# Dilated attention on one Trainium2 core: queries and keys split once for each head pair and sequence, with strided queries and keys laid by token mod 16

## What is computed

```python
DILATED_PATTERNS = ((128, 1), (512, 4), (2048, 16))

def dilated_window_attention(q, k, v, window, dilation):
    r = window // (2 * dilation)          # 64 for each of the three
    ...                                   # every dilation-th token forms a subsequence
    scores = jnp.einsum('nbqhd,nbkhd->nbhqk', qb, kw) * (HEAD_DIM ** -0.5)
    valid = (|qi - ki| <= r) & (ki >= 0) & (ki < l_sub)
    lse = jax.nn.logsumexp(scores, axis=-1)
    p = jnp.exp(scores - lse[..., None])
    o = jnp.einsum('nbhqk,nbkhd->nbqhd', p, vw)
    ...

def dilated_mixture(q, k, v):
    ...
    w = jax.nn.softmax(jnp.stack(lses, axis=0), axis=0)
    return jnp.sum(w[..., None] * jnp.stack(outs, axis=0), axis=0)
```

## Time and profile before

| | |
|---|---|
| median of 3 runs | 4136.37 us |
| lowest, highest | 4117.97, 4144.95 us |
| the profiled execution | 4143.03 us |
| its span, mean granted TensorE clock | 4141.0 us, 0.933 |
| TensorE busy over the span (products) | 3880.3 us, 94% |
| VectorE, ScalarE, GpSimd busy | 2095.0, 1547.7, 1498.9 us |
| attention, first score product to last output product | 2364.2 to 3490.6 us |

### The profile page before, as it was taken

The page is one execution under the profiler, slowest core; times in us unless marked ns, Lnnn a source line. Parts: engine busy times, 40 slices in busy tenths (PEclk is TensorE's granted clock), DMA queues, the critical chain, the costliest instruction groups (busy, mean ns, idle before and its releaser), DMA issues. The chain is left out here.

```text
span 4141.0 us, 62154 instructions
## 1 busy us (share of the span) xinstructions
PE 3880.3 (94%) x24989; PEld 3348.6 (81%) x24989; DVE 2095.0 (51%) x3847; ACT 1547.7 (37%) x2855; POOL 1498.9 (36%) x796
## 2 busy tenths in 40 slices
PE   6999999899889999999999799999999997799998
PEld 5877777677668998998988688888888886588887
DVE  2101278887324443444444355666656553467775
ACT  3323222121103222222222355777767664233322
POOL 1211155776553443343433433444433332211110
PEclk9999999999999999999999877999979885899999
DMA  6444245767533335334443223443334333454442
GB/s 233 134 158 174 83 150 189 277 219 269 171 120 112 117 105 194 110 117 146 149 122 110 88 64 101 120 122 106 94 102 122 91 83 105 151 185 172 178 181 107
DMA packets 431313, 582.99 MB, mean 141 GB/s; under 512 B 26155, under 2 KB 346739, under 8 KB 425395
## 3 DMA queue, kind: packets, MB, share of 16 engines
q1 hardware_dynamic: 425267, 562.23, 42.4%
q0 software_dynamic: 3456, 12.58, 0.7%
q10 hardware_dynamic: 2304, 4.20, 0.3%
HBM read 369.09 MB, written 209.83 MB: 140 GB/s over the span
## 5 line engine op out<-in xcount | busy, mean ns | idle before, releaser
L225 POOL TENSOR_TENSOR project_w_lo<-project_raw,project_w_hi 128x1024 fp32r<-128x1024 f32 (+1 forms) x204 | 434.8, 2141 | 1083.5 <-ACT project_w_hi L216 1083.5
L1668 ACT ACTIVATE attn_p_sb<-attn_p_sb,attn_o_sb 128x256 f32<-128x256 f32 (+1 forms) x1152 | 450.9, 464 | 335.7 <-DVE attn_o_sb L1703 335.6
L1634 PE MATMUL attn_o_ps<-attn_v,attn_pt_sb 128*128 128x65 f32 x3840 | 565.3, 305 | 0.0
L1634 PEld LDWEIGHTS attn_o_ps<-attn_v,attn_pt_sb 128*128 128x128 f32 x3840 | 522.4, 217 | 36.2 <-DVE attn_pt_sb L1713 2.7
L1713 DVE COPY attn_pt_sb<-attn_pt_ps 128x1024 f32<-128x1024 f32 (+1 forms) x288 | 301.5, 1047 | 376.8 <-PE attn_pt_ps L1618 376.7
L1703 DVE CUSTOM_DVE_ANT_0 attn_p_sb<-attn_mask,attn_s_ps 128x256 f32<-128x256 bf16 (+1 forms) x1152 | 363.9, 372 | 118.3 <-PE attn_s_ps L1606 117.2
L285 PE MATMUL third_out<-project_w_hi,project_h_hi 128*128 128x256 f32 x2304 | 373.9, 305 | 24.2 <-PEq L687 14.4
L285 PEld LDWEIGHTS third_out<-project_w_hi,project_h_hi 128*128 128x128 f32 x2304 | 301.6, 191 | 93.0 <-issue 84.9
L285 PE MATMUL third_out<-project_w_lo,project_h_hi 128*128 128x256 f32 x2304 | 326.6, 285 | 0.0
L285 PE MATMUL third_out<-project_w_hi,project_h_lo 128*128 128x256 f32 x2304 | 324.6, 284 | 0.0
L1510 POOL TENSOR_TENSOR attn_k_lo<-attn_nat,attn_k_hi 128x1024 fp32r<-128x1024 f32 (+1 forms) x96 | 199.5, 2078 | 338.0 <-ACT attn_k_hi L1658 337.9
(11 more groups left out here) (189 smaller groups left out, 6926.5 us busy)
## 6 DMA issues: line engine op xcount, KB each, us to landing
project_raw<-w_in SPq DMA_DIRECT2D x156, 512.0 KB, 5.9
output_parts<-s_o SPq DMA_DIRECT2D x24, 1584.0 KB, 6.5
s_o<-attn_o_sb SPq DMA_DIRECT2D x256, 132.0 KB, 2.0
s_xbcT<-first_stage SPq DMA_DIRECT2D x72, 256.0 KB, 2.1
project_h_hi<-s_h SPq DMA_DIRECT2D x8, 2048.0 KB, 8.9
project_h_lo<-s_h SPq DMA_DIRECT2D x8, 2048.0 KB, 13.7
s_xb<-second_toks SPq DMA_DIRECT2D x30, 512.0 KB, 6.7
second_xb<-s_xb SPq DMA_DIRECT2D x24, 640.0 KB, 9.9
```

Of the source, the lines that this page charges most:

```text
L225: last = nc.gpsimd.tensor_tensor(low, src, high.bitcast(F32), ALU.subtract)
L1634: last = nc.tensor.matmul(o_ps[n % 2][:, x, :], pt_sb[n % 2][:, x, b * P:(b + 1) * P], v[st.buf][:, st.chunk(r, t, b), half * VW:(half + 1 ...
L1668: last = nc.scalar.activation(cut, cut, ACT.Exp, scale=-1.0, bias=o_sb[n % ring][:, x % 2, x // 2, VW:OW])
```

## The change

Queries and keys are split once for each pair and sequence, 6 parts of 1024 tokens a pair, and all three dilations read the same split. For that the order becomes pair, sequence, dilation. The split queries lie in the order of the tokens, and a product takes them as its stationary operand with a stride of 1, 4, 16 or (short sequence, dilation 16) 8 elements. The split keys lie by token modulo 16 (`RHO`), 16 rows of 64 or 128 tokens with 16 of padding at either side; a product reads them as its moving operand in runs of 8 (dilation 1), 32 (dilation 4), 64 or 128 elements (dilation 16). So the keys of a block come in another order than before, and the masks (8 strips instead of 5) and the rows of the values follow it: the values of a banded stretch are loaded in 16 transfers, of 8 partitions each for dilation 1 and of 32 for dilation 4. The store of the short sequence at dilation 16 is one transfer. The splits of a sequence of the next pair are placed in the steps 1, 3, 5, 7 of the 12 steps of the short sequence, those of the pair's own short sequence at steps 4 and 8 of the long sequence. `load_nat` moves to the step i = 3 of dilation 16, behind the `load_v` of i = 2. TensorE waits for `a_low` only at the first step of a pair and sequence. The diff, cut to its core:

```diff
     def strip(self, t):
         if not self.banded:
-            return 3 + self.halves - 1
-        return 0 if t == 0 else 2 if t == self.tiles - 1 else 1
-
-    def query_at(self, r, t):
-        return (r * self.tiles + t) * P
-
-    def key_at(self, r, t):
-        return r * (self.tiles * P + 2 * self.pad) + t * P
+            return 6 + self.halves - 1
+        return 3 * self.pattern + (0 if t == 0 else 2 if t == self.tiles - 1 else 1)
+
+    def queries(self, q, rows, r, t):
+
+        step = self.dil // self.halves
+        by_sub = q[rows, :].rearrange("p (m r) -> p r m", r=step)
+        return by_sub[:, r, t * P:(t + 1) * P] if self.banded else by_sub[:, t, :]
+
+    def keys(self, k, rows, r, t):
+
+        if not self.banded:
+            own = k[rows, :, KPAD:KPAD + self.length // RHO].rearrange("p (h r) n -> p r h n", h=self.halves)
+            return own[:, t, :, :]
+        n = P * self.dil // RHO
+        first = KPAD + t * n - n // 2
+        own = k[rows, :, first:first + 2 * n].rearrange("p (q r) (b n) -> p r b q n", r=self.dil, b=2)
+        return own[:, r, :, :, :]
 
...
 def attention_stretches():
     stretches, first = [], 0
     for pair in range(PAIRS):
-        for pattern in range(len(DILATIONS)):
-            for s in (1, 0):
+        for s in (1, 0):
+            for pattern in range(len(DILATIONS)):
                 stretches.append(Stretch(len(stretches), pair, s, pattern, first))
...
+class Part:
+
+
+    def __init__(self, number, pair, s, which, half):
+        self.number, self.pair, self.s, self.which, self.half = number, pair, s, which, half
+        self.first = which == 0 and half == 0
+
+    def cut(self, t):
+
+        size = SEQS[0]
+        if self.which == 0:
+            return t[:, self.half * size:(self.half + 1) * size].rearrange("p (n r) -> p r n", r=1)
+        n = size // RHO
+        return t[:, :, KPAD + self.half * n:KPAD + (self.half + 1) * n]
+
+    def source(self, nat):
+        size = SEQS[0]
+        return nat[:, self.which, self.half * size:(self.half + 1) * size].rearrange(
+            "p (n r) -> p r n", r=RHO if self.which else 1)
+
+
+def attention_parts():
+    parts = []
+    for pair in range(PAIRS):
+        for s in (1, 0):
+            for which in range(2):
+                for half in range(SEQS[s] // SEQS[0]):
+                    parts.append(Part(len(parts), pair, s, which, half))
+    return parts
...
+        firsts = {(st.pair, st.s): st for st in stretches if st.pattern == 0}
+        ready = {}
         splits_at = [[] for _ in steps]
-        for st, following in zip(stretches, stretches[1:]):
-            for piece in range(pieces):
-                splits_at[max(0, st.first - 2 + piece * (2 if st.steps > pieces else 1))].append((following, piece))
+        for part in parts:
+            ready[(part.pair, part.s)] = part.number + 1
+            at = part.half + part.which * SEQS[part.s] // SEQS[0]
+            if part.s == 0:
+                splits_at[firsts[(part.pair, 1)].first + 4 + 4 * at].append(part)
+            elif part.pair:
+                splits_at[firsts[(part.pair - 1, 0)].first + 1 + 2 * at].append(part)
...
+            def narrow(strip, base, by_query, by_key):
+                pool.wait_ge(sem["a_mask_steps"], len(done) + 1)
+                dims = by_key + [[0, 1]] * (3 - len(by_key))
+                width = dims[0][1] * dims[1][1] * dims[2][1]
+                cut = mask[:, strip, 0:width].rearrange("p (b q n) -> p b q n", b=dims[0][1], q=dims[1][1])
+                nc.gpsimd.affine_select(out=cut, in_=cut, compare_op=ALU.is_ge, fill=BIG, base=base, pattern=dims,
                                         channel_multiplier=by_query).then_inc(sem["a_mask_steps"], 1)
-            cuts = (mask[:, 0, 0:BAND], mask[:, 2, 2 * P - BAND:2 * P], mask[0:BAND, 4, BAND:P], mask[BAND:P, 4, 0:BAND])
-            for n, cut in enumerate(cuts):
-                pool.wait_ge(sem["a_mask_steps"], len(rules) + 1 + n)
-                nc.gpsimd.memset(cut, BIG).then_inc(sem["a_mask_steps"], 1)
-            c["a_mask_total"] = len(rules) + 1 + len(cuts)
+                done.append(strip)
+
+            done = []
+            for pattern in range(2):
+                q, n = RHO // DILATIONS[pattern], P * DILATIONS[pattern] // RHO
+                after_key = [[P, 2], [1, q], [q, n]]
+                before_key = [[-P, 2], [-1, q], [-q, n]]
+                for strip in range(3 * pattern, 3 * pattern + 3):
+                    narrow(strip, 0, -1, after_key)
+                    narrow(strip, P, 1, before_key)
+                narrow(3 * pattern, -BAND, 0, after_key)
+                narrow(3 * pattern + 2, P + BAND - 1, 0, before_key)
+            narrow(6, BAND, -1, [[1, P]])
+            narrow(6, BAND, 1, [[-1, P]])
+            c["a_mask_total"] = len(done) + 1
...
                     reach = BAND * st.dil
-                    rows = cut[base - reach:base + st.length + reach, :].rearrange("(t p r) n -> r p t n", p=P, r=st.dil)
+                    m = P * st.dil // RHO
+                    rows = cut[base - reach:base + st.length + reach, :].rearrange(
+                        "(t m q r) n -> r q m t n", q=RHO // st.dil, m=m, r=st.dil)
                     for r in range(st.dil):
                         at = r * (st.tiles + 1)
-                        sp.dma_start(v[st.buf][:, at:at + st.tiles + 1, :], rows[r]).then_inc(sem["a_v_in"][st.buf], 16)
+                        for q in range(RHO // st.dil):
+                            sp.dma_start(v[st.buf][q * m:(q + 1) * m, at:at + st.tiles + 1, :], rows[r, q]
+                                         ).then_inc(sem["a_v_in"][st.buf], 16)
                 else:
-                    rows = cut[base:base + st.length, :].rearrange("(p t h) n -> h p t n", t=st.tiles, h=st.halves)
+                    rows = cut[base:base + st.length, :].rearrange("(p h t) n -> h p t n", t=st.tiles, h=st.halves)
...
-                    cut = P // st.halves
-                    for h in range(st.halves):
-                        dst = rows.rearrange("(p t h) n -> h p t n", t=st.tiles, h=st.halves)[h][:, t:t + 2, :]
-                        sp.dma_start(dst, src[h * cut:(h + 1) * cut, :, :, :].rearrange("p a h d -> p a (h d)")
-                                     ).then_inc(sem["a_stored"][n % ring], 16)
-
-            load_nat(stretches[0])
+                    dst = rows.rearrange("(p t) n -> p t n", t=st.tiles)[:, t:t + 2, :]
+                    sp.dma_start(dst, src[:, :, :, :].rearrange("p a h d -> p a (h d)")).then_inc(sem["a_stored"][n % ring], 16)
+
+            load_nat(0, 1)
             load_v(stretches[0])
-            load_nat(stretches[1])
+            load_nat(0, 0)
             for n, (st, i) in enumerate(steps):
                 if i == 2 and st.number + 1 < len(stretches):
                     load_v(stretches[st.number + 1])
-                if i == 0 and st.pattern == 2 and st.number + 2 < len(stretches):
-                    load_nat(stretches[st.number + 2])
-                if st.steps > pieces and i == 1:
+                if i == 3 and st.pattern == 2 and st.s == 1:
+                    load_nat(st.pair + 1, 1)
+                if i == 3 and st.pattern == 2 and st.s == 0:
+                    load_nat(st.pair + 1, 0)
...
-                if i == 0:
-                    pe.wait_ge(sem["a_low"], pieces * (st.number + 1))
+                if i == 0 and st.pattern == 0:
+                    pe.wait_ge(sem["a_low"], ready[(st.pair, st.s)])
 
                 after(pe, sem["a_max"], 4 * (n - 1))
                 terms = ((q_hi, k_hi), (q_hi, k_lo), (q_lo, k_hi))
                 for a, (r, t) in enumerate(st.tiles_of(i)):
-                    queries = slice(st.query_at(r, t), st.query_at(r, t) + P)
-                    keys = slice(st.key_at(r, t), st.key_at(r, t) + st.width)
                     for x, (qs, ks) in enumerate(terms):
                         for half in range(2):
                             rows = slice(64 * half, 64 * half + 64)
-                            last = nc.tensor.matmul(s_ps[n % 2][:, 2 * half + a, 0:st.width], qs[st.buf][rows, queries],
-                                                    ks[st.buf][rows, keys], start=x == 0, stop=x == 2)
+                            keys = st.keys(ks[st.s], rows, r, t)
+                            last = nc.tensor.matmul(s_ps[n % 2][:, 2 * half + a, 0:st.width],
+                                                    st.queries(qs[st.s], rows, r, t), keys, start=x == 0, stop=x == 2)
```

## The result

| | before | after |
|---|---|---|
| median, us | 4140.66 (4 runs) | 4288.15 (4 runs, 4264 to 4338) |
| ratio, 95% interval | | 1.0399 [1.0333, 1.0464] |
| the profiled execution, us | 4143.03 | 4300.86 |
| attention, first score product to last output product, us | 1126.4 | 1266.1 |
| TensorE's wait before the first score product, us | 27.3 | 39.0 |

The change makes the kernel 4% slower, where no change was forecast. Executions of one kernel differ by their granted clock (the kernel before took 4079 to 4249 us at clocks of 0.952 to 0.905), so the ratio, and the medians and ratios of the experiments, take only those within 1.5% of a kernel's fastest: for the changed kernel three, with a median of 4275.45 us. Between the two profiled executions lie 157.8 us; 139.7 of them are in the attention window and 11.7 in the wait ahead of it.

The account below looks back on a forecast made before the run. TensorE bounds attention (1126.4 us, 28.7 of them stalls, some 164 lost to low clock). 4143.0 - 28.7 - 82 + 98 + 5 + 12 = 4147.3, less 6.7 to the median: 4141 us, no change; range 3990 to 4300.

Parts of the forecast that it names:

- Stalls of the splits: TensorE's waits inside attention for the low parts of the keys: all 28.7 us taken as gone.
- Strided load: Weight loads of queries in dilations 4 and 16 double at full clock: 119 us, weighted to 98.
- Value bursts: Values in 16 pieces on SyncE's queue delay the stores behind them: 12 us, between nothing and 38.
- T: The start of a step's transposes, from which the prediction counted when stores land and are due.
- Clock: Of 165 us lost to TensorE's low clock in attention, between all and none come back: half, 82.
- half: The share of the low-clock loss in attention taken to come back, 82 of 165 us.
- with none: 4206: The forecast's case in which none of the clock lost in attention comes back: 4206 us.
- Start: Ahead of the first score product, 18 mask selects instead of 4 and a strided key split: net +5 us.
- short steps fall to the low clock: Rival, chance 0.12: with double-length loads the steps of dilation 16 run at 1.2 GHz for good, 4267 us.
- The free load: Rival, chance 0.37: the strided weight load of queries costs nothing, 3986 to 4110 us.
- more than double: Rival, chance 0.08: the strided weight load costs more than double; fourfold gives 4328 us.

Follow-up runs that it names:

- e2_whole_values: The changed kernel with the values of a banded stretch loaded as before, in 1 or 4 transfers of 128 partitions, strided queries kept: 4167.93 us, ratio 1.0063.
- e7: The changed kernel with queries gathered anew per stretch, values as e4, and first steps waiting only for the masks of dilation 1: 4016.72 us, ratio 0.9792.
- e4: The changed kernel with the values of dilation 1 in 8 transfers of 16 partitions that lie 8 apart, same data: 4178.75 us, ratio 1.0108.
- e3_both: The changed kernel with queries read as 128 consecutive elements and whole value transfers as before: 3983.29 us, ratio 0.9624.
- e1_flat_queries: The changed kernel with each weight load of queries taking 128 consecutive elements, value pieces kept: 4161.90 us, ratio 1.0067.

## Why the prediction was wrong

- *Stalls of the splits* (-28.7): right. One wait is left, at the start.
- *Strided load* (+98, or 119 at full clock): right in kind, and nearly in size. The spacing is 0.22 to 0.23 us; the steps grow by 0.70 and 0.65 us instead of 0.60 and 0.64, 130 us in all. The nearest row, ScalarE's cast with its factor of 1.98, was the fit comparison.
- *Value bursts* (+12, bound above 38): **the step that failed.** The working took the burst as 8.5 us of issue with a store "2.0" us behind it, and put the landing of the values away with "at twice the 6.9 us of the whole load it would still end within 5 us of the burst". At the first hand-over the load took 23.2 us, more than three times, and the store behind it 12.9. The 2.0 us came from rows in which the queue's transfers were large and spread over all partitions; no row showed a transfer of 8 partitions, so its cost should have had a wide bound above, and it had 38. The 2 MB of queries and keys issued right behind were not in the sum either. The place was wrong too: by its terms, with doubled loads, the store of the hand-over was due 2 x 2.93 + 2 x 3.72 - 2.1 = 11.2 us after T and landed at 10.1, in time, and the "1" us late was a guess; all seven waits for values stand there. Measured, the pieces cost 108 us with strided loads and 179 without: 52.4 us of waits for values and 12.7 for probabilities in the profile, the rest for the most part lost clock. Without the pieces the change is at 4168 us (e2_whole_values), 27 above the forecast.
- *Clock* (-82): none of it came back, 343 us low against 344. It was placed between all and none as if it were a cost of its own; it follows the other terms. Without pieces and with strided loads 155 us are low, without either 29. The reading that a stall is the trigger holds for the kernel before: each of its 12 low stretches inside attention begins right behind a wait of 1.06 to 1.95 us for low parts (eight others had no such sequel). What "half" hid is that the new waits do the same (194 us low), and that steps with doubled loads lose the clock with no wait at all (143 us). The sentence "with none: 4206" was the fitting case, and with the measured sizes it becomes 4206 + 54 (stalls of 66 instead of 12) + 11 (load) + 9 (clock) + 7 (start) = 4287.
- *Start* (+5): 11.7. The rows of before gave selects of 840 and 295 ns for 768 and 128 elements, so 404 for 256, and the 18 were to take 7.1 us. They took 15.4:

```profile
2362.05 15.43 POOL L1530 TENSOR_SCALAR_AFFINE_SELECT attn_mask<-attn_mask 128x256 bf16<-128x256 bf16 x18
...
L1530 POOL TENSOR_SCALAR_AFFINE_SELECT attn_mask<-attn_mask 128x256 bf16<-128x256 bf16 x16 | 8.6, 538 | 2.3
L1530 POOL TENSOR_SCALAR_AFFINE_SELECT attn_mask<-attn_mask 128x128 bf16<-128x128 bf16 x2 | 4.4, 2192 | 0.3
```

  The sixteen of 256 elements take 0.63 us in dilation 1 (runs of 8) and 0.45 in dilation 4 (runs of 32). The two of 128, the smallest, take 2.19 us each, where the kernel before has 295 ns for the same size: `narrow` fills their pattern up behind with dimensions of one element, so that its innermost run is 1 long. The time goes with the number of runs here, which the line between two shapes left out; a pattern filled up in front was not tried. (The 0.86 us of e7's expectation is the mean over both kinds.)
- *The rival "short steps fall to the low clock"* (0.12, 4267) named a mechanism that is there, as e2_whole_values shows, but in 37% of the time of dilation 16, below the point from which it decides. It is worth some 40 to 55 us (51 - 13, or 185 - 130), and it adds to the bursts. The time fell near its 4267 mostly for another reason.
- *The free load* and *more than double* fell: the spacing decides both.

The range (3990 to 4300) took in the time only because these rivals stretched it, which is luck; the chance of slower, 0.37, was too low because the burst, the one operation without a like in the trace, was priced by its nearest row as though that were a bound.

## What to carry to other kernels

A re-layout that cuts one transfer into many is to be priced twice: by the issues on its queue, with all that stands behind them, and by the partitions that a piece reaches; e4 shows that the same rows can be had by cuts that cost next to nothing. A gain and a loss that both pass through TensorE's clock don't add: ask of each wait what clock follows it, and put transfers where steps are long and stores have slack. Splitting once is worth having (e3_both, 3.8%), if the operand that sets TensorE's pace stays contiguous.

## What the runs showed of the hardware that was not expected

- TensorE's clock can fall with no stall: 26.00 of 26.00 us busy, and 1.04 us transposes become 1.92 (e2_whole_values). What went ahead were score products with doubled loads; with contiguous loads (e1_flat_queries, e3_both) every fall inside attention stands at a wait.
- A weight load at a stride of 2 fp32 elements is free, at 3 a pair takes 0.18 us, from 4 on 0.22 to 0.23; a moving operand of 256 columns doubles at a stride of 2 already, and runs of 8 are free.
- At the first hand-over, 1105 KB come in 20.2 us in transfers of 8 neighbouring partitions, in 11.8 of 8 partitions 16 apart (9.8 of them issue), and in 5.9 of 16 partitions 8 apart.
- An issue on SyncE's queue takes 0.35 to 0.37 us for 8 neighbouring partitions, 0.61 for 8 that lie 16 apart and 0.64 to 0.65 for 16 that lie 8 apart.
- A select on GpSimd takes longer the shorter the innermost run of its pattern: 256 elements 447 ns in runs of 32 and 627 in runs of 8, and 128 elements 2192 ns in runs of 1, against 295 in one run.
